# State-space loop: two tiles interleaved, rotation and scan held in PSUM, half-array products alternated, first weights split inside the loop

## The reference, cut to what matters

```python
u = h.astype(f32).reshape(bsz, seqlen, SSM_GROUPS, SSM_GROUP)      # 64 groups of 16
bu_re = jnp.einsum('blgh,gph->blgp', u, bbar_re)                   # 64 complex states a group
bu_im = jnp.einsum('blgh,gph->blgp', u, bbar_im)
_, _, xr, xi = lax.associative_scan(_ssm_combine, (a_r, a_i, bu_re, bu_im), axis=1)
y = (jnp.einsum('ghp,blgp->blgh', c_re.astype(f32), xr)
     - jnp.einsum('ghp,blgp->blgh', c_im.astype(f32), xi))
y = y.reshape(bsz, seqlen, D_MODEL) + d.astype(f32) * h.astype(f32)
y = jax.nn.gelu(y).astype(h.dtype)
val, gate = jnp.split(y @ w_out, 2, axis=-1)
```

## Time and profile before

| | |
|---|---|
| median of three runs | 2998.43 us |
| the profiled execution | 3000.43 us |
| its span | 2998.6 us |
| preparation, loop, entry, rest | to 119, to 323, to 330, to the end |
| PE, DVE, ACT, POOL busy over the span | 91%, 52%, 33%, 6% |
| mean granted clock of TensorE | 0.936 of 2.4 GHz |

### The profile page before, as it was taken

How to read it: one execution, slowest core, us unless ns; L and a number is a source line. 1 busy time by engine, 2 the same in 40 slices (tenths; PEclk the granted TensorE clock), 3 DMA queues, 4 the chain that set the end, 5 groups by cost and what they waited for, 6 DMA issues and landing times.

```text
span 2998.6 us, 34092 instructions
## 1 busy us (share of the span) xinstructions
PE 2737.4 (91%) x14144; PEld 2230.4 (74%) x14144; DVE 1563.3 (52%) x2132; ACT 980.9 (33%) x1237; POOL 165.6 (6%) x154
## 2 busy tenths in 40 slices
PE   1478789999999999998999999989999898899996
PEld 0356668888788788887888888778887787688885
DVE  7776464555545433336555555463335665653435
ACT  1011232222322322225555555332223464332221
POOL 4265000000000000000000000000000000000000
PEclk7566899999999999999999999999999889899998
DMA  4100434454133132313222222122222122132220
GB/s 172 70 16 16 188 120 189 181 212 161 67 102 124 67 112 85 110 66 99 64 85 64 75 75 86 70 84 85 106 91 77 43 71 71 56 113 85 95 102 28
DMA packets 43525, 283.58 MB, mean 95 GB/s; under 512 B 5985, under 2 KB 6113, under 8 KB 16754
## 3 DMA queue, kind: packets, MB, share of 16 engines
q1 hardware_dynamic: 38018, 243.15, 22.9%
q0 software_dynamic: 5360, 38.31, 3.3%
HBM read 279.35 MB, written 2.10 MB: 94 GB/s over the span
## 4 chain that ended last, share of the span: by engine, by line
PE 84%; DVE 11%; ACT 3%; issue 1%; DMA 0%; SPq 0%; DVEq 0%; ACTq 0%
PE PS L513 20%; PE PS L514 20%; PE PS L515 20%; PE PS L605 4%; PE PS L607 3%; PE PS L606 3%; PE PS L486 2%; PE PS L686 1%; PE PS L626 1%; PE PS L627 1%; PE PS L628 1%; PE PS L674 1%; PE PS L493 1%; DVE Wl L1152 1%; DVE raw L1173 1%
## 5 line engine op out<-in xcount | busy, mean ns | idle before, releaser
L513 PE MATMUL PS<-Hl,Wh 128*128 128x512 f32 x1536 | 609.3, 397 | 43.9 <-DVE Hl L1481 23.7
L514 PE MATMUL PS<-Hh,Wl 128*128 128x512 f32 x1536 | 604.9, 394 | 0.0
L515 PE MATMUL PS<-Hh,Wh 128*128 128x512 f32 x1536 | 604.0, 393 | 0.0
L513 PE MATMUL PS<-Gl,Wh 128*128 128x512 f32 x1152 | 457.2, 397 | 9.6 <-DVE Wl L1152 9.6
L846 ACT CAST Wh<-raw 128x2048 fp32r<-128x2048 f32 (+2 forms) x182 | 320.7, 1810 | 425.7 <-PE PS L515 403.9
L515 PE MATMUL PS<-Gh,Wh 128*128 128x512 f32 x1152 | 456.0, 396 | 0.0
L514 PE MATMUL PS<-Gh,Wl 128*128 128x512 f32 x1152 | 455.9, 396 | 0.0
L1152 DVE TENSOR_TENSOR Wl<-raw,Wh 128x2048 fp32r<-128x2048 f32 (+2 forms) x182 | 387.6, 2171 | 91.7 <-ACT Wh L846 91.7
L513 PEld LDWEIGHTS PS<-Hl,Wh 128*128 128x128 f32 x1536 | 293.1, 191 | 112.7 <-issue 51.0
L514 PEld LDWEIGHTS PS<-Hh,Wl 128*128 128x128 f32 x1536 | 293.3, 191 | 62.8 <-issue 1.6
L515 PEld LDWEIGHTS PS<-Hh,Wh 128*128 128x128 f32 x1536 | 292.9, 191 | 62.0
(11 more groups left out here) (383 smaller groups left out, 3462.8 us busy)
## 6 DMA issues: line engine op xcount, KB each, us to landing
raw<-wstream SPq DMA_DIRECT2D x156, 1024.0 KB, 5.4
raw<-wstream SPq DMA_DIRECT2D x64, 768.0 KB, 4.4
adab<-adaw POOLq DMA_DIRECT2D x36, 1024.0 KB, 5.7
raw<-adaw SPq DMA_DIRECT2D x12, 1024.0 KB, 4.8
raw<-wstream SPq DMA_DIRECT2D x12, 512.0 KB, 4.3
X<-xT SPq DMA_DIRECT2D x1, 2048.0 KB, 9.9
XU<-xU SPq DMA_DIRECT2D x1, 2048.0 KB, 18.3
yT<-X SPq DMA_DIRECT2D x1, 2048.0 KB, 6.3
```

The source lines that it names most:

```text
L513: mm(o, Wh[:, s, c0:c0 + P], xl[:, k, :], start=k == 0, stop=False)
L514: mm(o, Wl[:, s, c0:c0 + P], xh[:, k, :], start=False, stop=False)
L515: last = mm(o, Wh[:, s, c0:c0 + P], xh[:, k, :], start=False, stop=k == kt - 1)
```

## The change

TensorE runs `s5_transposes` (split off `s5_lags`) one tile ahead. Carried-in products of t come before the convolution of t, right behind the lags of t, and increments of t+1 follow them. DVE computes states(t+1) in iteration t, before y(t) is known, and the low part of t-1. Rotations and scan have one operand and the result in PSUM (banks 4 and 6), and sine and cosine products are 512 wide. D u goes into Kf's diagonal, so that GELU reads PSUM (bank 7 or 0, alternating). ACT takes over the bias of u (`s5_u`), scale and bias of U (eight instructions of 64 columns, `s5_uu`) and the Bb copy. POOL's negation is replaced by a table `nC`, and its order is F(t+1), E(t). Products of half the rows alternate e in the inner loop; the carried-in ones now write both halves of one bank, and the output transposes are 16 of 64 x 64 instead of 8 of 64 x 128. The four modulation products of the loop stand in tiles 0 to 3. Pair 0 is split by ACT after Gh of tile 6 and its low part made by DVE after states(7); SBUF is laid out anew so that it does not hit buffers in use.

```diff
@@ tensor @@
             for t in range(KT):
+                if t + 1 < KT:
+                    s5_transposes(t + 1)
+                s5_lags(t)
+                pe.wait_ge(s5_s["xin"], t + 1)
+                if t:
+                    pe.wait_ge(s5_s["yi"], t)
+                for i in range(4):
+                    for c in range(2):
+                        for e in range(2):
+                            r = slice(64 * e, 64 * e + 64)
+                            last = mm(PS[r, 5, i * P:(i + 1) * P], Xin[r, c, i, 0:NC_S5], Et[r, b, c, 1:9, i, :], start=c == 0, stop=c == 1)
+                last.then_inc(s5_s["inter"], 1)
+                if t + 1 < KT:
+                    s5_increments(t + 1)
                 pe.wait_ge(s5_s["kf"], t + 1)
-                if t:
-                    pe.wait_ge(s5_s["yv"], t)
-                yp = PS[:, 7, :].rearrange("p (c j) -> p c j", j=CL)
+                pe.wait_ge(s5_s["us"], t + 1)
+                if t >= 2:
+                    pe.wait_ge(s5_s["gh"], t - 1)
+                yp = PS[:, y_bank(t), :].rearrange("p (c j) -> p c j", j=CL)
...
-                if t + 1 < KT:
-                    s5_lags(t + 1)
...
                 pe.wait_ge(s5_s["yi"], t + 1)
                 for j in range(CL):
-                    last = mm(yp[:, :, j], Yi[:, j, :, :].rearrange("p g h -> p (g h)"), ident[0:64, 0:64], start=False, stop=j == CL - 1, skip_group_check=True)
+                    for e in range(2):
+                        r = slice(64 * e, 64 * e + 64)
+                        last = mm(yp[r, :, j], Yi[r, j, :, :].rearrange("p g h -> p (g h)"), ident[r, 64 * e:64 * e + 64],
+                                  start=False, stop=j == CL - 1, skip_group_check=True)
@@ scalar @@
+                nc.scalar.copy(Bb[:, t % 2].rearrange("p c (i h) -> p c i h", i=4), Ft[:, t % 2, :, :, 0, :]).then_inc(s5_s["bb"], 1)
+            def s5_u(t):
+                act.wait_ge(s5_s["xr"], t + 1)
+                A(u_s[:, t % 2, :], u_s[:, t % 2, :], ACT.Identity, bias=AB_f[:, 1, t:t + 1]).then_inc(s5_s["us"], 1)
+            def s5_uu(t):
+                act.wait_ge(s5_s["xu"], t + 1)
+                for g in range(8):
+                    last = A(U_s[:, t % 2, g, :], U_s[:, t % 2, g, :], ACT.Identity, scale=AB_U[:, g, t:t + 1], bias=AB_U[:, g, 8 + t:9 + t])
+                last.then_inc(s5_s["u"], 1)
...
+                o.link(A(yg[:, :], PS[:, y_bank(t), :], ACT.Gelu_apprx_tanh))
                 nc.scalar.copy(Gh[:, t, :], yg[:, :]).then_inc(s5_s["gh"], 1)
+                if t == KT - 2:
+                    split(0, half_width(0))
@@ vector @@
+                STT(Kf[:, 0, :], ident, S5D[:, t:t + 1], Kf[:, 0, :], ALU.mult, ALU.add).then_inc(s5_s["kf"], 1)
+            def s5_states(t):
...
+                S, Q = (PS[:, bank, :].rearrange("p (x n) -> p x n", x=2) for bank in (4, 6))
                 dve.wait_ge(s5_s["inc"], t + 1)
+                step(TT(Q, S, co, ALU.mult))
+                step(TT(rt[:, :, :], S, si, ALU.mult))
                 sync()
+                step(TT(Q[:, 0], Q[:, 0], rt[:, 1], ALU.add))
+                step(TT(Q[:, 1], Q[:, 1], rt[:, 0], ALU.subtract))
+                sync()
                 for c in range(2):
-                    step(V_.tensor_tensor_scan(WW[:, c], rho, ZZ[:, c], 0.0, ALU.mult, ALU.add))
+                    step(V_.tensor_tensor_scan(S[:, c], rho, Q[:, c], 0.0, ALU.mult, ALU.add))
                 sync()
+                step(TT(Q, S, co, ALU.mult))
+                step(TT(rt[:, :, :], S, si, ALU.mult))
...
+            s5_states(0)
+            for t in range(KT):
+                s5_kf(t)
                 if t + 1 < KT:
                     s5_u(t + 1)
                 if t + 2 < KT:
                     s5_uu(t + 2)
                 if t:
+                    s5_low(t - 1)
+                if t < 4:
+                    ada(8 + t)
...
+                if t + 1 < KT:
+                    s5_states(t + 1)
+                if t == KT - 2:
+                    low(0, half_width(0))
+            s5_low(KT - 1)
@@ gpsimd @@
+            s5_f(0)
+            for t in range(KT):
+                if t + 1 < KT:
+                    s5_f(t + 1)
+                s5_e(t)
```

More of the change, by code:

```diff
@@ L124, in build @@
         ftmp = sb("ftmp", [P, 2, 4, 8, 16], c=s5)
+        nC = sb("nC", [P, 2, 32, 16], c=s5)
         Bb = sb("Bb", [P, 2, 2, 64], c=s5)
+        tw = sb("tw", [P, 2, 32], c=s5)
+        AB_U = sb("AB_U", [P, 8, 16], c=s5)
+        S5A = sb("S5A", [P, 3, 32], c=s5)
+        BM = sb("BM", [P, 64], c=s5)
+        prmi = sb("prmi", [P, 32], I32, c=s5)
+        XU = sb("XU", [P, 64, NC_S5], c=s5)
+        BC = sb("BC", [P, 4, 32, 16], c=s5)
+        RHO = sb("RHO", [P, 32, NC_S5], c=s5)
+        CS = sb("CS", [P, 2, 32, NC_S5], c=s5)
+        bada_s = sb("bada_s", [P, 48], c=s5)
+        c_act = sb("c_act", [P, D], c=s5)
+        GS = sb("GS", [P, 8, P], c=s5)
+        JS = sb("JS", [1, 8, P], c=s5)
+        prm = sb("prm", [P, 24, 32], c=s5)
+        AP_ = sb("AP_", [P, 2, 9, 32], c=s5)
+        QP = sb("QP", [P, 2, 8, 32], c=s5)
+        PW = sb("PW", [P, 2, 6, 32], c=s5)
+        AB_f = sb("AB_f", [P, 2, KT], c=s5)
+        RU = sb("RU", [P, NC_S5], c=s5)
         FT = sb("FT", [P, 2, 4, P], c=s5)
@@ L249, in build @@
             "fir", "mods", "cact", "ab", "sel", "rn", "ru", "abu", "tab", "e", "f", "tr", "ftc", "kx", "kf", "inc",
-            "xin", "inter", "yi", "y", "yv", "g", "gh", "gl", "u", "prm_a", "prm_v")}
+            "xin", "inter", "yi", "y", "gh", "gl", "xr", "us", "xu", "u", "bb", "nc", "prm_a", "prm_v")}
         lb_diff, lb_done = sem("lb_diff"), sem("lb_done")
@@ L456, in s5_increments @@
                 for i in range(4):
-                    for e in range(2):
-                        for c in range(2):
+                    for c in range(2):
+                        for e in range(2):
                             last = mm(PS[64 * e:64 * e + 64, 4, c * 256 + i * 64:c * 256 + i * 64 + 64],
@@ L572, in last_product @@
                 norm_sums(n, 4 * ((p + 1) % 2), ln)
+            pe.wait_ge(s5_s["gh"], KT - 1)
             for j in range(3):
@@ L1415, in add_square @@
                     TT(SQA, SQA, sq[:, k % 2, :], ALU.add).then_inc(nm_sa, 1)
-            low(0, half_width(0))
             for j in range(4):
@@ L1784, in _, with s5_f @@
             pord = sem("pool_ord")
-            pool.wait_ge(s5_s["tab"], 1)
-            for t in range(KT):
-                b = t % 2
-                i0 = 4 * t
-                TTg = g_.tensor_tensor
-                if t >= 2:
-                    pool.wait_ge(s5_s["kx"], t - 1)
+            TTg = g_.tensor_tensor
+            def s5_f(t):
+                b, i0 = t % 2, 4 * t
                 def qcoef(c):
```

146 lines of the change are left out of this document (64 added, 82 removed).

## The result

The changed kernel took 2912.72 us (median of four runs, 2907.17 to 2916.56) where the kernel before took 2998.52 us beside it: a ratio of 0.9712, 95% interval 0.9692 to 0.9732. The forecast was 2923, with 2902 to 2963 as its range. The profiled execution took 2909.12 us, its span is 2907.3 us.

What follows compares the result with a forecast made beforehand. POOL was taken to pace the loop once the serial chain went. First product at 114.1 (tile 0's transposes) + 140 = 254.1 instead of 329.67, gain 75.6, hence 2923 us against the median; range 2902 to 2963.

Steps and rivals of the forecast that it cites:

- the preparation's ladder of small DVE instructions: Before the loop: 14 small DVE instructions taking 7.0 us beside POOL would take 2.6 with POOL idle, gaining 4.3 us.
- Z: Start of tile 0's transposes, 119.35 us before the change; forecast 114.1, a gain of 5.2 us, bounds 0 and 6.
- States: DVE's rotation, scan, rotation back and Xin of one tile: forecast 6.4 us, between 5.8 clean and 12 contended.
- the slower rival: Results written to PSUM are slow themselves; gain ends at states of 15.7 us, else up to 3022 us; chance 0.04.
- below POOL: Loop pace: DVE's tile of 13.5 us, 17.5 with ada, stays under POOL's 16.7 and 18.4, so POOL sets the pace.
- E of tile 6: POOL's E instructions for tile 6, forecast done at Z+109.6, 8.4 us before E of tile 7.
- TensorE waits for E at each tile: Sign in the loop that POOL sets the pace, with E to E taking 16 to 18.5 us.
- E of tile 7: POOL's last E instructions in the loop, forecast done at Z+118.
- the 15 us of disturbance: Time POOL loses to DVE's SBUF use in the loop: 7.0 us for ada and 8 for the rest.
- the rivals 2970 and 3022: 2970 us: PSUM doesn't free DVE, states stay at 12 us, chance 0.04; 3022: results written to PSUM are slow, 0.04.
- TensorE waits some 5 us: Loop's tail: after inter(7), near Z+125, TensorE waits for Kf(7), queued on DVE behind low(0).
- The rival in which it sets the pace: TensorE paces the loop at 20.5 us a tile, halves not overlapping, clock mixed: gain 41.6, 2957 us; chance 0.18.

Runs made afterwards that it cites:

- serial: The changed kernel with the low part of y(t) made before the states of t+1, one chain again: first product 21.2 us later, 2938.13 us, ratio 0.9799 to before.
- sbuf: The changed kernel with results of the first rotation and the scan in SBUF again: first product 28.7 us later, 2938.11 us, ratio 0.9799 to before.
- before_pool_rest_b: The kernel before, with POOL held ahead of E of tile 1 until tile 0's transposes are done: transposes 6.5 us earlier, 2998.42 us, ratio 0.9996.
- kf_first_b: The changed kernel with weight pair 0's low part moved behind tile 7's lag matrix Kf: first product at 240.42 instead of 246.23, 2906.65 us, ratio 0.9693 to before.

## Why the prediction was right, and where it was not

**The direction and the mechanism held.** The serial chain went (serial: 21 us), DVE was freed by PSUM (sbuf: 29 us), the preparation's ladder of small DVE instructions shortened (before_pool_rest_b). Z, forecast 114.1, came at 113.79. States took 5.9 where 6.4 was forecast; writing to PSUM cost next to nothing (0.70 us at L1403, 0.68 into SBUF at L1404), which closes the slower rival. Taken back one at a time the four parts are 61 us, the preparation is 5.6; the other 17 (bias and copies on ACT, D u, POOL's shorter tile, and what the parts do together) were not tried singly.

**The step that failed is "below POOL": who sets the pace.** Both tile times were near: POOL 16.1 to 18.4 (forecast 16.7, 18.4), DVE 13.5 to 16.9 (13.5, 17.5). POOL is the slower one per tile, and yet DVE decides every tile, because POOL starts 13 us ahead and loses only 1 to 3 us a tile. The forecast compared rates and left out the lead, though it had both ends of it. By its own numbers (an estimate) E of tile 1 is done at about Z+16.6 (3.4 + 5.1 + 8.1), while the products of tile 1 stand at Z+31.9 (14.4 + 17.5); with 17.5 a tile up to tile 4 and 13.5 behind it DVE reaches tile 6 at Z+111.4, and POOL's E of tile 6, forecast for Z+109.6, with the lags behind it, at about Z+111: a tie. That the sum came out near, though it ran over the wrong engine, is owed to this tie, which is luck. The check "TensorE waits for E at each tile" is wrong in all eight.

**The terms.** E of tile 7 ended at Z+113.1 (forecast 118): the 15 us of disturbance were 10. E of tile 6 came at Z+104.9 (109.6); from it to the end of y(6) 11.5 us (12). The low part ended at Z+124.0 (129), Kf(7) followed in 1.8, the convolution took 5.7 from a low clock (6.0), the output 1.15 (2.8), and the first product came at Z+132.4 (140). So of the 7.9 us at that point some 5 had been gained by the end of y(6) (Z+116.4 for Z+121.6), with E of tile 6 4.7 early and DVE level with it; 1.7 are the output's, which took less than half, and the rest is small change. In the prices of the rivals 2970 and 3022 lack the 2 us from the profiled run to the median; it changes nothing. "TensorE waits some 5 us" for Kf(7) was 4.4, and kf_first_b shows that it was to be had for nothing.

**TensorE.** 11.6 us a tile at the high clock (forecast 10.3 to 14), at a granted 0.91 with gaps of 0.6 to 4.4 us ahead of the carried-in products. The rival in which it sets the pace fell. The slow carried-in products (3.37 at 143.06, granted 0.55 behind a gap of 4.40; 3.58 at 208.34, granted 0.52 behind 2.22) show that the clock can drop behind such gaps. It cost 1.5 to 1.6 us each time and not the tile: from 146.4 the granted clock was 0.96 again. Behind the first gap, 2.19 ahead of 127.44, it stayed at 1.00.

**Behind the first product** nothing was forecast, and the profiled executions differ by 7.9 us. A part is the clock: the first 100 us behind it were granted 0.99 instead of 0.96, since TensorE enters at the high level (0.40 us a product instead of 0.63), and at the first long gap, some 95 us on, the changed kernel is 1.8 us ahead. The rest shows at gaps further on (4.2 us by 1040 us behind the first product, 7.9 from about 2160), has no change of the program behind it, and the whole is inside the 10 us by which the same instructions scatter from kernel to kernel. It stays open, and no edit here should be credited with it.

## What to carry to other kernels

Between two engines that feed a third, compare not only their times per tile but the lead of the slower one and how much it loses a tile; the one that is faster per tile can still be the one that is waited for, and adding work to each in turn shows which. Where DVE works beside GpSimd, count each DVE instruction's inputs in SBUF: one of two moved to PSUM is worth about a microsecond at 512 columns, more here than the reordering of the loop. Work that is put early into an in-order queue goes behind what is needed next, not ahead of it.

## What was not expected of the hardware

- A DVE instruction with two SBUF inputs that waited for GpSimd paid about 0.9 us, nearly whatever its size: 128 columns took 1.21 to 1.33 for 0.35 (three of the eight in the changed kernel), 512 columns 1.57 on average for 0.69, 1024 columns 2.20 for 1.22. Small ones are hit hardest in proportion, and in the preparation some copies and TENSOR_SCALARs with one SBUF input were hit too.
- The same instructions took 2661 to 2671 us behind the first product. A difference of 0.2% between single executions of such kernels says nothing; the start of a fixed instruction early in the trace scatters by about 1 us and so resolved shifts of 2 us.
- Alternating the array halves brought 1.7 times the speed for products of 64 and 128 columns, and nothing for 512.
